# Value projection of the first layer on columns of x that are not yet normalised

## What is computed

```python
def rms_norm(x, gain):
    y = x * rsqrt(mean(x * x, axis=-1) + EPS)
    return y * gain
...
u = rms_norm(h, norm_pre[layer])                    # h is the input x in layer 0
proj = u @ w_in                                     # q, k, v, g: 1024 columns each; fl: 16 columns
log_f = log_sigmoid(fl + b_f); c = cumsum(log_f)    # the forget bias of the attention
...
mod = silu(c_2) @ w_ada_2 + b_ada_2                 # used in the second block, needs no x
```

## Time and profile before

| what | value |
|---|---|
| three runs | 1721.20, 1717.59, 1720.95 us; median 1720.95 |
| the profiled execution's own time | 1722.19 us |
| its span, first instruction to last | 1720.4 us |
| PE busy | 1601.9 us (93%) |
| DVE busy | 820.3 us (48%) |
| ACT busy | 618.8 us (36%) |
| POOL busy | 590.0 us (34%) |
| DMA | 157.11 MB, mean 91 GB/s |

### The profile page before, as it was taken

One profiled execution on the slowest core, in us unless ns is written; L12 is line 12 of the kernel. 1 busy time (PEld: TensorE's weight loads), 2 busy tenths in 40 slices (PEclk: granted clock), 3 DMA queues, 4 the chain that ended last, 5 costly groups with the idle time before them and its releaser, 6 DMA issues.

```text
span 1720.4 us, 22854 instructions
## 1 busy us (share of the span) xinstructions
PE 1601.9 (93%) x9177; PEld 1242.7 (72%) x9177; DVE 820.3 (48%) x1504; ACT 618.8 (36%) x1106; POOL 590.0 (34%) x452
## 2 busy tenths in 40 slices
PE   5899999999999889699899999999999899999997
PEld 4788766787788566577677776666677778777786
DVE  3788356333334346633608995424364632222224
ACT  4222465452322243534324324554343322212222
POOL 2445111243444221225143432221244254444441
PEclk9998999999999999899999999999999999999999
DMA  6867110232223110124131221200123233232221
GB/s 241 293 223 243 50 50 26 68 104 74 75 97 98 54 50 27 50 75 134 49 115 55 93 90 50 64 25 25 49 74 111 82 102 98 98 98 89 85 97 74
DMA packets 85289, 157.11 MB, mean 91 GB/s; under 512 B 2704, under 2 KB 20672, under 8 KB 85184
## 3 DMA queue, kind: packets, MB, share of 16 engines
q1 hardware_dynamic: 81184, 146.81, 25.7%
q10 hardware_dynamic: 4000, 8.84, 1.5%
HBM read 153.52 MB, written 2.12 MB: 90 GB/s over the span
## 4 chain that ended last, share of the span: by engine, by line
PE 74%; DVE 13%; ACT 5%; issue 3%; DMA 2%; POOL 2%; PEld 1%; DVEq 0%; SPq 0%; ACTq 0%; PEldq 0%
PE banks L360 10%; PE banks L361 9%; PE banks L362 9%; PE banks L356 8%; PE banks L358 7%; PE banks L357 7%; PE banks L469 3%; PE banks L470 3%; PE banks L471 3%; PE banks L746 2%; PE banks L494 2%; PE banks L509 2%; PE banks L519 2%; DVE slots L1655 2%; DVE max L1653 2%
## 5 line engine op out<-in xcount | busy, mean ns | idle before, releaser
L334 POOL TENSOR_TENSOR w_lo<-w_raw,w_hi 128x512 fp32r<-128x512 f32 x448 | 589.8, 1350 | 1100.0 <-ACT w_hi L825 1099.9
L825 ACT ACTIVATE w_hi<-w_raw 128x2048 fp32r<-128x2048 f32 (+1 forms) x114 | 214.6, 1882 | 221.0 <-DMA w_raw<-w_ff_dram 152.8
L356 PE MATMUL banks<-xh,w_hi 128*128 128x512 f32 x640 | 252.0, 394 | 5.0 <-issue 4.0
L358 PE MATMUL banks<-xh,w_lo 128*128 128x512 f32 x640 | 249.7, 390 | 0.0
L357 PE MATMUL banks<-xl,w_hi 128*128 128x512 f32 x640 | 249.7, 390 | 0.0
L360 PE MATMUL banks<-w_hi,xh 128*128 128x512 f32 x384 | 158.4, 413 | 24.9 <-POOL w_lo L334 12.3
L360 PE MATMUL banks<-w_hi,yh 128*128 128x512 f32 x384 | 151.4, 394 | 6.5 <-issue 4.2
L361 PE MATMUL banks<-w_lo,xh 128*128 128x512 f32 x384 | 154.2, 402 | 0.0
L362 PE MATMUL banks<-w_hi,xl 128*128 128x512 f32 x384 | 153.9, 401 | 0.0
L362 PE MATMUL banks<-w_hi,yl 128*128 128x512 f32 x384 | 149.7, 390 | 0.0
L361 PE MATMUL banks<-w_lo,yh 128*128 128x512 f32 x384 | 149.7, 390 | 0.0
(11 more groups left out here) (298 smaller groups left out, 2412.6 us busy)
## 6 DMA issues: line engine op xcount, KB each, us to landing
w_raw<-w_ff_dram SPq DMA_DIRECT2D x32, 1024.0 KB, 5.3
w_raw<-w_in_dram SPq DMA_DIRECT2D x22, 1024.0 KB, 5.1
w_raw<-att_w_in_dram SPq DMA_DIRECT2D x16, 1024.0 KB, 7.8
work_hi<-w_ada_dram SPq DMA_DIRECT2D x16, 1024.0 KB, 7.4
w_raw<-rec_w_in_dram SPq DMA_DIRECT2D x16, 1024.0 KB, 5.3
work_lo<-w_ada_dram SPq DMA_DIRECT2D x8, 1024.0 KB, 6.8
w_raw<-ple_w_gate_dram SPq DMA_DIRECT2D x8, 1024.0 KB, 5.1
w_raw<-att_w_out_dram SPq DMA_DIRECT2D x4, 1024.0 KB, 5.1
```

What stands on the lines that cost most here:

```text
L334: ins = pool.tensor_tensor(wlo[s][:, k, :], raw[s][:, k, :], wh[s][:, k, :].bitcast(F32), ALU.subtract)
L356: pe.matmul(out, w_h, x_h, start=start, stop=False)
L358: return pe.matmul(out, w_l, x_h, start=False, stop=stop)
L825: act.activation(wh[s][:, 0:kn, :], raw[s][:, 0:kn, :], ACT.Copy).then_inc(w_split, 1)
```

## The change

The host gives x a second time, transposed (`c_x_cols`), and the gain of the first norm as 8 columns. SP loads the columns and weight chunks 0 and 1 in alternating pieces of two contraction tiles (512 KB each), then x by rows in one load. ACT makes the high half of column tile k times gain, and of weight tile k; DVE and POOL the low halves; PE runs tv0 by contraction tile k, 12 matmuls each, into four banks that stay open. ACT multiplies by the inverse root of the token when it empties the banks of tv0 and v0. The four transposes of x, the normalised rows and their splits are gone.

The later projections need normalised columns. PE spreads the inverse roots over a bank, as a row (four small matmuls after the first tile of v0); DVE multiplies the 8 column tiles with gain and that row (L1546), and splits them a second time: tiles 0 to 3 after the first half of v0 is done, tiles 4 to 7 token tile by token tile after each bank of v0 (L1552 to L1558). Ada chunks 0 to 3 stand before that multiplication, 4 and 5 behind it. fl0 waits for the second split. In SP's list the ada chunks stand in another pattern between the weight chunks.

```diff
--- before.py
+++ after.py
@@ STAGES @@
-    ("tv0", TV, 2, 0, 0), ("v0", "AAAA", 2, 0, 0), ...
+    ("tv0", "AAAA", 2, 0, 0), ("v0", "AAAA", 2, 0, 0), ...
@@ tiles @@
-        small = sb("small_columns", [P, P])
+        small = sb("small_columns", [P, P + KT])
+        gain0 = small[:, P:P + KT]
...
+        x_cols = feat["D"]
@@ SP @@
-            for t in range(TT):
-                sp.dma_start(h[:, t, :], a["x"][0][t * P:t * P + P, :]).then_inc(sg(f"x_in{t}"), 16)
-                if t % 2:
-                    load(cols(win0, first[0], k0=4 * (t // 2)))
-            for c in range(24):
-                load_ada(c)
-                if c % 2 and count[0] < 12:
-                    load(cols(win0, first[count[0] // 2], k0=4 * (count[0] % 2)))
+            for j in range(4):
+                sp.dma_start(x_cols[:, 2 * j:2 * j + 2, :], a["c_x_cols"][2 * j * P:2 * (j + 1) * P, :].rearrange("(k p) t -> p k t", p=P))\
+                  .then_inc(sg(f"first_in{j}"), 16)
+                s = slot_of() if j % 2 == 0 else j // 2
+                sp.dma_start(raw[s][:, 2 * (j % 2):2 * (j % 2) + 2, :], cols(win0, first[0], k0=2 * j, kn=2))\
+                  .then_inc(w_landed[s] if j % 2 else sg(f"first_in{j}"), 16)
+            sp.dma_start(h[:, :, :], a["x"][0].rearrange("(t p) d -> p t d", p=P)).then_inc(sg("x_in"), 16)
+            n_ada = 0
+            for adas in (0, 3, 3, 1, 2, 3, 4, 4, 4, 0):
+                for _ in range(adas):
+                    load_ada(n_ada)
+                    n_ada += 1
+                load(cols(win0, first[count[0] // 2], k0=4 * (count[0] % 2)))
@@ POOL (and every wait on w_ready / w_split: the count is two lower) @@
-                pool.wait_ge(w_split, c + 1)
+                if c < 2:
+                    for k in range(4):
+                        pool.wait_ge(sg("first_hi"), 2 * (4 * c + k) + 2)
+                        pool.tensor_tensor(wlo[s][:, k, :], raw[s][:, k, :], wh[s][:, k, :].bitcast(F32), ALU.subtract).then_inc(sg("v_lo"), 1)
+                    continue
+                pool.wait_ge(w_split, c - 1)
@@ PE @@
-            pe.wait_ge(const_in, 48)
-
-            norm_and_values("tv0", sg("tv0_xn"))
-            groups("v0", 1, False)
+            n0 = BASE["tv0"][0]
+            for k in range(KT):
+                pe.wait_ge(sg("x_lo"), k + 1)
+                pe.wait_ge(sg("v_lo"), k + 1)
+                for m in range(TT):
+                    mm = three(bank(n0 + m), k // 4, k % 4, xh, xl, k, m, False, k == 0, k == KT - 1)
...
+                if k == 3:
+                    mm.then_inc(w_free, 1)
+            pe.drain().then_inc(w_free, 1)
+
+            def row_of_roots(ch, m):
+
+                if ch == 0 and m == 0:
+                    pe.wait_ge(const_in, 16)
+                    pe.wait_ge(*emptied(n0))
+                    for t in range(TT):
+                        mm = pe.matmul(ps[:, 0, t * P:t * P + P], stat[:, 32 + t:33 + t].broadcast_to([P, P]), ident[:, :], start=True, stop=True)
+                    mm.then_inc(sg("row_full"), 1)
+
+            groups("v0", 1, False, between=row_of_roots)
             n = BASE["fl0"][0]
             pe.wait_ge(sg("fl_split"), 1)
             wait_bank(n)
             for k in range(KT):
+                if k % 4 == 0:
+                    pe.wait_ge(sg("x_lo"), 12 + k)
@@ ACT @@
+            act.dma_start(small[:, :], a["c_small"]).then_inc(sg("small_in"), 16)
             act.dma_start(ident[:, :], a["c_ident"]).then_inc(const_in, 16)
-            act.dma_start(small[:, :], a["c_small"]).then_inc(const_in, 16)
-            act.dma_start(g_row, a["norm_pre"][0].partition_broadcast(P)).then_inc(const_in, 16)
+            act.wait_ge(sg("small_in"), 16)
+            A.after(act.activation(stat[:, 40:48], c_col, ACT.Silu))
+            act.sem_inc(sg("c_silu"), 1)
+            for k in range(KT):
+                act.wait_ge(sg(f"first_in{k // 2}"), 32 if k % 4 < 2 else 16)
+                act.activation(xh[:, k, :], x_cols[:, k, :], ACT.Copy, scale=gain0[:, k:k + 1]).then_inc(sg("first_hi"), 1)
+                if k % 4 == 2:
+                    act.wait_ge(w_landed[k // 4], 16)
+                act.activation(wh[k // 4][:, k % 4, :], raw[k // 4][:, k % 4, :], ACT.Copy).then_inc(sg("first_hi"), 1)
...
+            act.wait_ge(sg("x_in"), 16)
+            for m in range(TT):
+                square("tv0", h[:, m, :], stat[:, 8 + m:9 + m], to=tok["A"][:, m, :])
+                root("tv0", stat[:, 32 + m:33 + m], stat[:, 8 + m:9 + m], eps)
+            high(2)
+            high(3)
+            act.wait_ge(sg("tv0_inv"), TT)
+            for m in range(TT):
+                empty(BASE["tv0"][0] + m, tok["C"][:, m, 0:G], scale=stat[:, 32 + m:33 + m])
+            high_after("v0", 0)
+            for m in range(TT):
+                empty(BASE["v0"][0] + m, tok["C"][:, m, G:D], scale=stat[:, 32 + m:33 + m])
+            high_after("v0", 1)
@@ DVE @@
-            dve.wait_ge(const_in, 48)
-            n = BASE["tv0"][0]
-            whole_rows("tv0", 0, g_row)
-            whole_rows("tv0", 1, g_row)
-            lows("tv0", n + TV_T[0], 0)
...
+            dve.wait_ge(sg("small_in"), 16)
+            for k in range(KT):
+                dve.wait_ge(sg("first_hi"), 2 * k + 1)
+                dve.scalar_tensor_tensor(out=xl[:, k, :], in0=x_cols[:, k, :], scalar=gain0[:, k:k + 1], in1=xh[:, k, :].bitcast(F32),
+                                         op0=ALU.mult, op1=ALU.subtract).then_inc(sg("x_lo"), 1)
+            for m in range(TT):
+                dve.wait_ge(sg("tv0_root"), m + 1)
+                dve.reciprocal(stat[:, 32 + m:33 + m], stat[:, 32 + m:33 + m]).then_inc(sg("tv0_inv"), 1)
+            dve.wait_ge(sg("c_silu"), 1)
+            modulation(0, 2)
+            dve.wait_ge(sg("row_full"), 1)
+            for k in range(KT):
+                V.mark(dve.scalar_tensor_tensor(out=x_cols[:, k, :], in0=x_cols[:, k, :], scalar=gain0[:, k:k + 1], in1=ps[:, 0, :],
+                                                op0=ALU.mult, op1=ALU.mult))
+            V.wait()
+            modulation(2, 3)
+            dve.wait_ge(w_free, 3)
+            for k in range(4):
+                V.after(dve.tensor_copy(xh[:, k, :], x_cols[:, k, :]))
+                dve.tensor_tensor(xl[:, k, :], x_cols[:, k, :], xh[:, k, :].bitcast(F32), ALU.subtract).then_inc(sg("x_lo"), 1)
+            for m in range(TT):
+                x, x_h, x_l = (y[:, 4:8, m * P:m * P + P] for y in (x_cols, xh, xl))
+                dve.wait_ge(bank_full, BASE["v0"][0] + m + 1)
+                V.after(dve.tensor_copy(x_h, x))
+                dve.tensor_tensor(x_l, x, x_h.bitcast(F32), ALU.subtract).then_inc(sg("x_lo"), 1)
+            dve.wait_ge(sg("x_lo"), 16)
             dve.wait_ge(sg("fl_in"), 16)
             V.after(dve.tensor_copy(wfl_h[:, :, :], wfl))
...
-            modulation()
+            modulation(3, 12)
+            modulation_columns()
```

More of the change, by code:

```diff
@@ L55 @@
 STAGES = [
-    ("tv0", TV, 2, 0, 0), ("v0", "AAAA", 2, 0, 0), ("fl0", "A", 0, 0, 0), ("q0", "A" * 8, 4, 0, 0), ("ka0", "AAAA", 2, 0, 0),
+    ("tv0", "AAAA", 2, 0, 0), ("v0", "AAAA", 2, 0, 0), ("fl0", "A", 0, 0, 0), ("q0", "A" * 8, 4, 0, 0), ("ka0", "AAAA", 2, 0, 0),
     ("ada_a", "A", 0, 0, 0), ("kb0", "AAAA", 2, 0, 0), ("ada_b", "A", 0, 0, 0), ("g0", "", 4, 0, 0),
@@ L362, in three, with group @@
                 return pe.matmul(out, x_l, w_h, start=False, stop=stop)
-            def group(n, c, feature_major, act_h=xh, act_l=xl, a0=0, chunks=2, kn=4, ready=None, tile_ready=None):
+            def group(n, c, feature_major, act_h=xh, act_l=xl, a0=0, chunks=2, kn=4, ready=None, tile_ready=None, between=None):
                 for ch in range(chunks):
-                    pe.wait_ge(w_ready, c + (ch + 1))
+                    pe.wait_ge(w_ready, c + (ch - 1))
                     for m in range(4):
@@ L385, in group @@
                             mm.then_inc(w_free, 1)
+                        if between:
+                            between(ch, m)
             def group_by_halves(n, c, act_h, act_l, tile_ready=None):
@@ L576, in out_and_ple @@
                     pe.wait_ge(sg("mod_ready"), 1)
-                    pe.transpose(bank(n)[:, 0:P], small[:, :], ident[:, :]).then_inc(bank_full, 1)
+                    pe.transpose(bank(n)[:, 0:P], small[:, 0:P], ident[:, :]).then_inc(bank_full, 1)
                 groups(f"outb{l}", 1, False, act_h=yh, act_l=yl)
@@ L1026, in _ @@
             act.dma_start(grow[:, :], a["norm_post"][0].partition_broadcast(P)).then_inc(sg("grow0"), 16)
-            act.wait_ge(const_in, 48)
-            A.after(act.activation(stat[:, 40:48], c_col, ACT.Silu))
-            act.sem_inc(sg("c_silu"), 1)
             act.preload_act_table_set("sqrt_and_others")
[L1031 to L1040, removed]
+            act.wait_ge(sg("x_in"), 16)
[11 more added lines that the diff above has]
+            high_after("v0", 1)
             n = BASE["fl0"][0]
```

(22 more changed lines are left out.)

11 lines of the change are left out of this document (7 added, 4 removed).

## The result

The changed kernel takes 1732.82 us (median of 4 runs, 1731.1 to 1734.13), the kernel before on the same chip 1719.97 (4 runs). The ratio is 1.007, with a 95% interval of 1.0058 to 1.0082: it is slower by 12 us. The forecast was 1732.6.

The account below looks back on a forecast made before the run. PE was taken to bound the kernel, busy 93% of the span. A 1.0 us gain at fl0, then waits of 5.5 and 4.2 us with 1.5 of clock loss each, gave +11.7: 1732.6 us, own range 1727 to 1738.

Parts of the forecast that it names:

- PE's start: First value matmul at 8.4 us instead of 23.59; tv0 then ends at about 32 us.
- v0's end: v0 ends at 58.5 us, before near 79: a gain of 20 us if PE can go on.
- The DVE list: DVE's work ahead of fl0: 35.4 us plus 12.8 lost to POOL, from 28.1 to 76.3 us.
- Rivals A: POOL does not hold DVE up this much; fl0's split ends at 63.5 us, 1713 us in all; chance 0.14.
- C: DVE and POOL take strict turns, costing DVE 19.6 us instead of 12.8; 1740 us in all; chance 0.09.
- fl0's end: fl0 takes 5.4 + 1.5 us and ends at 83.2, before at about 84.2: a gain of 1.0 us.
- Weight chunk 8: Behind ada chunk 15, ready at 132.8 us, wanted at 127.3: PE waits 5.5 us and loses 1.5 by the clock.
- Weight chunk 9: Behind ada chunk 19, ready at 149.4 us, wanted at 145.2: PE waits 4.2 us and loses 1.5 by the clock.
- Rival B: Waits for weight chunks 8 and 9 do not come, as DVE finishes ada chunks sooner; 1720 us; chance 0.07.
- The sum: Whole kernel: -1.0 + 5.5 + 1.5 + 4.2 + 1.5 = +11.7 us, giving 1732.6 us.
- Rival D: fl0's wait is short and v0's 20 us mostly survive, less the two waits; 1708 us; chance 0.04.
- The rule on turns: Trainium skill's exclusive lock on the port pair DVE and POOL share; the loss would be 6.8 us above the rows' figure.

Follow-up runs that it names:

- e9: Changed kernel with one edit: ACT empties tv0's four banks ahead of the high half of weight chunk 3. 1732.14 us, ratio 1.0058.
- e1: Changed kernel with SP's list from weight chunk 8 on as before the change (two ada chunks ahead of each weight chunk). 1722.57 us, ratio 1.0006.
- e3: Changed kernel without the second split; layer 0's forget columns, queries, keys and gate use columns not normalised. 1717.75 us, ratio 0.9985.
- e2: Kernel before the change with only the changed kernel's SP list from weight chunk 8 on. 1734.88 us, ratio 1.0077.
- e6: Changed kernel with DVE's list reordered (fl0's split first, ada chunks 2 on later) and two ada chunks between weight chunks in SP's list. 1705.95 us, ratio 0.991.
- e8: e6 with one more edit: ACT empties tv0's four banks ahead of the high half of weight chunk 3. 1701.57 us, ratio 0.9883.
- e4: Changed kernel with ada chunks 4 and 5 behind the second split and the split for fl0. 1727.62 us, ratio 1.0035.

## Why the prediction was right, point by point

- **PE's start.** Forecast 8.4 us, measured 9.31: the first weight piece was there at 6.4, not 5.9, and POOL began at 7.74. tv0 ended at 34.0 us, not at 32: for its first 6 us the matmuls started 0.43 us apart, then 0.23, so the slow start cost 3 us and not 1.5.
- **v0's end.** Forecast 58.5; the last bank was read at 60.29 us. The row of roots came at 40.05 (38.8 forecast), eight small matmuls in 1.1 us, where 0.5 had been guessed. e9 shows that the time of the row does not count.
- **The DVE list.** Forecast from 28.1 to 76.3 us, measured 28.54 to 77.50. The terms: six ada chunks 18.6 without POOL's share against 28.5 with it; multiplications 5.6 against 5.36; second split 9.2 against 12.3; the split for fl0 2.0 against 2.0. The loss to POOL, 12.8 us in the forecast, is 13.6 by the same sum (49.0 us of list less 35.4, 0.8 of it small gaps), and most of it falls on the ada chunks. Rivals A (it loses little) and C (19.6) are out.
- **fl0's end.** This step was off: forecast 1.0 us sooner than before, measured 1.5 later (ACT reads fl at 86.25 us, before at 84.72). 1.2 us are the DVE list. The rest is the clock: I had charged 1.5 us behind every wait, from 3.3 us at the low clock. Here it stayed low for 6 us, as the first row below shows (two stretches of the changed kernel by engine, columns as for e1).

```profile
77.60:85.00 7.40, 7.39 (x20) 5.90 (x21) 6.25 (x12) 0.00 (x0) 0.00 (x0) 0.59 0.38 118
134.50:147.30 12.80, 12.77 (x48) 10.10 (x48) 10.80 (x15) 1.92 (x1) 2.31 (x2) 0.87 0.90 321
```

At 0.59 over 7.4 us, some 6 us of them were at 1.2 GHz, and fl0 took 8.4 us and not 6.9. The length of the wait does not explain it: ahead of the same fl0, a wait of 20.35 us in e9 was followed by 3.0 us at 0.50, and one of 3.30 us in e3 by 5.6. What decides it stays open here. The second row is the first half of ka0: 12.8 us instead of 10.9, so 1.9 and not 1.5 behind that wait.
- **Weight chunk 8.** Forecast: issued at 116.8, ready 132.8, a wait of 5.5 us. Measured: issued at 118.97, ready 134.44, a wait of 4.28, since PE came 2.9 us later than forecast as well.
- **Weight chunk 9.** Forecast: ready at 149.4, a wait of 4.2. Measured: ready at 151.03, a wait of 3.82. Rival B (no such waits) is out by e1 and e2.
- **The sum.** 1.5 + 4.28 + 1.9 + 3.82 + 1.9 = 13.4 us; the attention came 12.6 later. The 0.8 between them are three small things: 0.26 us of the first wait is a gap that PE has there before the change too, the halves of ka0 took 11.0 us each before and not 10.9, and the part from the first ada sum to the attention is 0.3 shorter. Forecast 11.7, measured 12.85 by the medians. The errors (fl0 2.5 too low, the waits 1.6 too high, the clock 0.8 too low) partly cancel, and the kernel before ran 1.0 us lower in the runs of the result than in those of the forecast, so the hit of 1732.6 to 0.2 us is luck; the mechanism is not.
- **Rival D** (the front's gain survives) is wrong for this kernel, but e6 and e8 show what it takes: the 20 us from v0 were there to be had, and 15 to 20 us came through once DVE's order and SP's list let them.

The rule on turns weighed in the prediction: beside POOL, DVE's 128x512 subtractions with two SBUF tensors took 1.63 to 1.67 us also in these runs, and POOL's four instructions 5.7 to 6.5 us. By strict turns, an estimate from the lock that the Trainium skill describes ("SBUF — State Buffer", "Who interferes with whom"), these would be 2.0 and 8. That page also exempts a DVE instruction with at most one SBUF input, outside DVE's two-port modes, and there the trace agrees: 5.36 us for the eight multiplications, with POOL beside the first 3 us and without it. It does not exempt casts, which it counts among the instructions that can enter those modes, and the trace agrees there too: 0.42 us alone, up to 1.53 beside POOL.

## What to carry to other kernels

When a front is made shorter, ask what the next step waits for, and list every instruction that now stands ahead of it on that engine. Here PE had its first 24 us cut by 14, and handed them all to DVE's list.

In a queue that is taken in order, a load that depends on nothing late (the weights) must not stand behind loads that a slow consumer releases (the ada chunks). Moving two or four such loads ahead of a 1 MB chunk cost 4 to 5 us of waiting each time, and nearly 2 us of low clock behind it.

Place DVE instructions with two SBUF operands, and casts, where POOL rests, and those with a PSUM operand where it works.

## What the runs showed that was not expected

- Beside POOL tiny DVE instructions take almost as long as 128x512 casts (1.2 to 1.5 us): the four steps on `lb_cols` (128 by 8 or 16 elements) take 0.17 us each in the changed kernel, where POOL is idle, and 1.14 to 1.22 us for three of them in e6 and e8, where POOL works. The kernel before had shown it already (1.03 to 1.21 us beside weight chunk 3). DVE's timeline of the changed kernel, and then of e6:

```profile
77.85 0.17 DVE L1566 TENSOR_TENSOR lb_cols<-lb_cols 128x8 f32<-128x8 f32 x1
```

```profile
67.22 1.22 DVE L1568 TENSOR_TENSOR lb_cols<-lb_cols 128x8 f32<-128x8 f32 x1
```

- How long the clock stays low behind a wait does not follow the wait. It was at 0.50 for 6.0 us after 17.36 us of waiting (changed kernel), 3.0 after 20.35 (e9), 6.05 after 9.84 (e4), 5.6 after 3.30 (e3) and 3.3 after 4.79 (before). At half speed that is 1.5 to 3 us lost per wait, so a flat 1.5 is the low end.
- The part behind the first attention, the same program in all kernels, needed between 1524.9 and 1531.9 us in the eleven profiles. A difference of 3 us between two single profiles says nothing here; such a difference has to be read at the attention's start or from the runs.
